# The sums of the down weights, made by GpSimd during the input projections instead of in prompt attention

## The reference, cut to what matters

```python
z = x @ w_in + b_in                       # GLU, q latent, kv latent, rope key, two gates
u, conv_state = causal_dwconv(conv_prev, a * sigmoid(g), conv_dw_w, conv_dw_b)   # width 31
y_conv = silu(layer_norm(u)) @ w_conv_out
...
mix = (g_conv * y_conv + g_mla * y_mla) @ w_mix_out   # y_mla: latent attention, prompt, then samples
x1 = layer_norm(ALPHA * x + mix)
h, ffn_state = causal_dwconv(ffn_prev, x1 @ w_up, ffn_dw_w, ffn_dw_b)            # width 3
f = (silu(hg) * hv) @ w_down              # w_down: 2816 x 1024
y = layer_norm(ALPHA * x1 + f)
```

## Time and profile before

| | |
|---|---|
| time, median of three runs | 2009.12 us (2006.18 to 2009.48) |
| the profiled execution's own time | 2004.44 us |
| its span, first to last instruction | 2002.6 us |
| mean granted clock of TensorE | 0.992 of full speed |
| busy in the span | PE 97%, PEld 89%, DVE 69%, ACT 42%, POOL 45% |
| moved by DMA | 264.08 MB, 132 GB/s on the mean |

### The profile page before, as it was taken

The page is one execution under the profiler, slowest core; times in us unless marked ns, Lnnn a source line. Parts: engine busy times, 40 slices in busy tenths (PEclk is TensorE's granted clock), DMA queues, the critical chain, the costliest instruction groups (busy, mean ns, idle before and its releaser), DMA issues.

```text
span 2002.6 us, 34425 instructions
## 1 busy us (share of the span) xinstructions
PE 1938.3 (97%) x13332; PEld 1782.6 (89%) x13332; DVE 1377.1 (69%) x1808; ACT 840.1 (42%) x1482; POOL 910.4 (45%) x562
## 2 busy tenths in 40 slices
PE   9999999999998999998999999989999999999998
PEld 8999999999997888886667999889999999977776
DVE  3999999956636647655445323798887777746778
ACT  4222222225335666674334121654544344554441
POOL 4812334421212343124330235678787878645542
PEclk9999999999999999999999999999999999999999
DMA  6422222323541333326573432242232222468655
GB/s 220 152 95 75 86 95 86 100 82 134 163 137 64 128 122 118 101 92 250 216 280 110 152 115 88 85 133 91 81 106 75 86 76 86 134 197 306 198 184 177
DMA packets 203535, 264.08 MB, mean 132 GB/s; under 512 B 22221, under 2 KB 142303, under 8 KB 199277
## 3 DMA queue, kind: packets, MB, share of 16 engines
q1 hardware_dynamic: 185600, 189.38, 29.6%
q0 software_dynamic: 8320, 46.27, 6.0%
q10 hardware_dynamic: 9469, 26.36, 3.5%
HBM read 200.25 MB, written 62.57 MB: 131 GB/s over the span
## 4 chain that ended last, share of the span: by engine, by line
PE 78%; DVE 10%; issue 3%; DMA 3%; ACT 3%; POOL 2%; SPq 1%; ACTq 0%; DVEq 0%; POOLq 0%
PE ps L2739 32%; PE ps L3394 14%; PE ps L3475 6%; PE ps L2932 5%; PE pst L3394 5%; PE pst L3475 2%; PE ps L3146 2%; PE ps L3199 1%; PE pst L3178 1%; DMA tw_d<-wraw 1%; PE pst L3011 1%; POOL tw_raw L1784 1%; DVE hv L2493 1%; PE pst L3181 1%; DVE tfr L2477 1%
## 5 line engine op out<-in xcount | busy, mean ns | idle before, releaser
L1710 POOL TENSOR_TENSOR wlo<-wraw,whi 128x1024 fp32r<-128x1024 f32 x66 | 160.4, 2435 | 388.2 <-ACT whi L981 293.3
L1986 DVE SCALAR_TENSOR_TENSOR pst<-g_ext,wtap,pst 128x512 f32<-128x512 f32 x464 | 306.9, 751 | 0.0
L2739 PE MATMUL ps<-xh,whi 128*128 128x352 f32 x864 | 187.1, 325 | 1.2 <-ACT stat L1075 1.2
L2739 PE MATMUL ps<-xh,wlo 128*128 128x352 f32 x864 | 186.2, 323 | 0.0
L2739 PE MATMUL ps<-xl,whi 128*128 128x352 f32 x864 | 186.0, 323 | 0.0
L2739 PEld LDWEIGHTS ps<-xh,whi 128*128 128x128 f32 x864 | 147.0, 189 | 1.9 <-issue 1.8
L2739 PEld LDWEIGHTS ps<-xh,wlo 128*128 128x128 f32 x864 | 148.3, 188 | 0.0
L2739 PEld LDWEIGHTS ps<-xl,whi 128*128 128x128 f32 x864 | 146.7, 188 | 0.0
L1880 POOL TENSOR_TENSOR wlo<-wraw,whi 128x512 fp32r<-128x512 f32 x60 | 90.8, 1520 | 33.1 <-ACT whi L1501 33.1
L1880 POOL TENSOR_TENSOR wlo<-x1f,whi 128x512 fp32r<-128x512 f32 x60 | 88.4, 1480 | 36.7 <-ACT whi L1501 36.7
L3394 PE MATMUL ps<-resr,whi 128*128 128x264 f32 x480 | 98.0, 286 | 0.0
(11 more groups left out here) (527 smaller groups left out, 5745.7 us busy)
## 6 DMA issues: line engine op xcount, KB each, us to landing
inr<-f_d SPq DMA_DIRECT2D x77, 256.0 KB, 4.1
wraw<-in_w_in SPq DMA_DIRECT2D x37, 512.0 KB, 3.8
f_d<-hv SPq DMA_DIRECT2D x22, 528.0 KB, 2.7
wraw<-in_w_up SPq DMA_DIRECT2D x40, 256.0 KB, 3.7
x1f<-in_w_up SPq DMA_DIRECT2D x40, 256.0 KB, 3.7
wraw<-in_w_down SPq DMA_DIRECT2D x27, 256.0 KB, 4.1
wraw<-tw_d SPq DMA_DIRECT2D x24, 256.0 KB, 3.8
tw_raw<-in_w_down SPq DMA_DIRECT2D x11, 512.0 KB, 3.5
```

The lines of the kernel that those rows point to most:

```text
L1710: nc.gpsimd.tensor_tensor(wlo[:, n % HL, :], wraw[:, n % RAW, :], whi[:, n % HL, :].bitcast(F32), ALU.subtract).then_inc(lo_done, 1)
L1986: half[x] = link(nc.vector.scalar_tensor_tensor(out=dst, in0=src, scalar=tap(k_), in1=pst[:, x, :], op0=ALU.mult, op1=ALU.add))
L2739: last = nc.tensor.matmul(out[:, c, 0:CH], w[:, k, :], x[:, k, c * CH:(c + 1) * CH], start=(k == 0 and x is hi_x and w is wh), stop=(k == ...
```

## The change

The sums move from prompt attention into the input projections. GpSimd makes those of two inner tiles in each tile m: k = 2m - 1 behind `lo(4m + 1)` and k = 2m behind `lo(4m + 3)`, from k = 0 at the end of tile 0 to k = 10 at the end of tile 5. The four subtractions are the same. The blocks lie in one buffer `tw` of four blocks, which covers the end of the place of `u`, the convolution's output (part of its tile 6 and its tile 7), so ScalarE now waits, in tile 6 before it writes the gate for VectorE, until all sums are stored. SyncE's loop over the tiles is written out, and in it loads (two transfers of 512 KB) and stores (one of 1 MB) stand between the loads of `w_in`. Semaphores that were shared with the old place are given back, and others are shared with the new one. In `tw_d` the four results have another order, which the loads of the down product follow.

```diff
-        tw_raw = at("tw_raw", [P, 2, NH], F32, X0 + 29568)
-        tw_low = wraw[:, (N2 + 1) % RAW, NH:2 * NH]
-        tw_high = at("tw_high", [P, NH], F32, R0 + 8192 + (N2 + 1) % HL * 4096 + 2048)
+        tw = at("tw", [P, 4, NH], F32, R1 + 2 * XB + 25600)
...
-            with sp.Fori(1, MT) as m:
+            w_dn = A["w_down"]
+
+            def w_down_blocks(k):
+                if k == 0:
+                    sp.wait_ge(tr_read, 1)
+                else:
+                    sp.wait_ge(ffn_out, 16 * k)
+                for j in range(2):
+                    r = (k + j * KH) * P
+                    sp.dma_start(tw[:, 2 * j:2 * j + 2, :], two(w_dn[0, r:r + P, :])).then_inc(gb2_in, 16)
+
+            def w_down_sums(k):
+                sp.wait_ge(xc_done, 4 * (k + 1))
+                sp.dma_start(tw_d[k].rearrange("j p n -> p j n"), tw[:, :, :]).then_inc(ffn_out, 16)
+
+            for m in range(1, MT):
                 for t in range(4):
-                    sp.wait_ge(lo_done, 4 * m + (t + 1))
-                    sp.dma_start(slot3(wraw, t % RAW), w_in_v[:, :, bass.ds(m * P + gate_cols[t], P)]
-                                 ).then_inc(raw_in[t % RAW], 16)
+                    load(4 * m + t, w_in_v[:, :, m * P + gate_cols[t]:(m + 1) * P + gate_cols[t]])
+                    k = 2 * (m - 1) + t // 2
+                    if k < KH:
+                        if t % 2:
+                            w_down_sums(k)
+                        else:
+                            w_down_blocks(k)
                 sp.wait_ge(wm_out, 16 * m)
-                sp.dma_start(wrow[:, :], A["w_mix_out"][0, bass.ds(m * P, P), :]).then_inc(wr_in, 16)
+                sp.dma_start(wrow[:, :], A["w_mix_out"][0, m * P:(m + 1) * P, :]).then_inc(wr_in, 16)
...
-                if h == 1:
-                    w_down_blocks(0)
-                if 1 <= h < 7:
-                    for k in range(2 * h - 2, min(2 * h, KH)):
-                        w_down_sums(k)
-                        if k + 1 < KH:
-                            w_down_blocks(k + 1)
-
-
-            sp.wait_ge(wm_out, TW_OUT)
...
-                    src = tw_d[k, {2: 0, 5: 1, 3: 2, 6: 3}[e]]
+                    src = tw_d[k, {2: 0, 5: 1, 6: 2, 3: 3}[e]]
...
                     elif t == 1:
+                        if m == MT - 2:
+                            act.wait_ge(ffn_out, TW_OUT)
                         nc.scalar.activation(split(sg[s][:, :]), acc(1), ACT.Sigmoid,
...
+            def w_down_sum(k, s, out, a, b):
+                if s < 2:
+                    pool.wait_ge(gb2_in, 32 * (k + 1))
+                else:
+                    pool.wait_ge(xc_done, 4 * k + s - (s == 2))
+                nc.gpsimd.tensor_tensor(out, a, b, ALU.subtract).then_inc(xc_done, 1)
+
+            def w_down_sums(k):
+                w11, w12, w21, w22 = (tw[:, j, :] for j in range(4))
+                w_down_sum(k, 0, w11, w12, w11)
+                w_down_sum(k, 1, w12, w22, w12)
+                w_down_sum(k, 2, w22, w22, w11)
+                w_down_sum(k, 3, w21, w21, w22)
+
             for m in range(MT):
                 for t in range(2):
                     lo(4 * m + t)
                     if m == 1:
                         x_tile(4 + t)
+                if 1 <= m < 6:
+                    w_down_sums(2 * m - 1)
...
                     if m == 1:
                         x_tile(6 + t)
+                if m < 6:
+                    w_down_sums(2 * m)
                 if m >= CSUM:
                     add_squares(max(1, m - 2))
...
-                if 1 <= h < 7:
-                    for k in range(2 * h - 2, min(2 * h, KH)):
-                        w_down_sums(k)
...
             pool.wait_ge(s_done, 8 * H)
-            pool.wait_ge(wm_out, TW_OUT)
```

More of the change, by code:

```diff
@@ L455, in program @@
         xb_in = sem("x_mean_in")
[L456 to L459, removed]
+        xc_done = sem("w_down_sum_steps_or_x_tile_centred")
+        wr_in = sem("w_mix_rows_in")
+        wm_c = sem("w_mix_centre_steps")
+        wm_out = sem("w_mix_rows_out")
         xr_out = sem("residual_stored")
@@ L471, in program @@
         f_in = x_in + ga_in + xt_in
-        gb2_in = sem("ln2_rows_in")
+        gb2_in = sem("w_down_blocks_or_ln2_rows_in")
         y_t = sem("down_product_tiles_done")
@@ L481, in program @@
         kf_r = sem("ffn_rows_read")
-        ffn_out = sem("ffn_state_out")
+        ffn_out = sem("w_down_sums_or_ffn_state_out")
         uses = [5, 4]
@@ L582, in program @@
         RS = {n: RS0 + j + 1 for j, n in enumerate(("11", "22", "samples", "12", "21"))}
-        TW_IN0, TW_C0, TW_OUT0 = 16 * MT, 3 * MT, 16 * MT
-        TW_OUT = TW_OUT0 + 48 * KH
+        TW_IN, TW_C, TW_OUT = 32 * KH, 4 * KH, 16 * KH
         UP_V0, UP_A0, F_HI0, F_LO0, SP_T0, SP_C0 = MT, MT, 2 * MT + 1, MT, 4, 6
@@ L710, in _ @@
             HQ = DN + DR
[L711 to L728, removed]
             for h in range(H):
@@ L969, in _ @@
             sp.wait_ge(orow_out[1], 32 * 4)
-            sp.wait_ge(ffn_out, 16 * (SG + 1))
+            sp.wait_ge(ffn_out, TW_OUT + 16 * (SG + 1))
             for j in range(4):
@@ L1777, in _ @@
                 lo(n)
-            def w_down_sum(k, s, out, a, b):
-                if s == 0:
-                    pool.wait_ge(wr_in, TW_IN0 + 48 * (k + 1))
-                elif s != 1:
-                    pool.wait_ge(wm_c, TW_C0 + 4 * k + (s - 1 if s == 2 else 3))
-                nc.gpsimd.tensor_tensor(out, a, b, ALU.subtract).then_inc(wm_c, 1)
-            def w_down_sums(k):
-                w_down_sum(k, 0, tw_raw[:, 0, :], tw_raw[:, 1, :], tw_raw[:, 0, :])
-                w_down_sum(k, 1, tw_raw[:, 1, :], tw_high[:, :], tw_raw[:, 1, :])
-                w_down_sum(k, 2, tw_high[:, :], tw_high[:, :], tw_raw[:, 0, :])
-                w_down_sum(k, 3, tw_low, tw_low, tw_high[:, :])
             for h in range(H):
@@ L2396, in _ @@
                 dve.wait_ge(w_used, N4 + m + HL + 1)
-                dve.wait_ge(xc_done, m + 1)
+                dve.wait_ge(xc_done, TW_C + m + 1)
                 residual(m, None, None).then_inc(free[q], 1)
@@ L2673, in normalise @@
                 if t == Y_TURN[0]:
-                    dve.wait_ge(gb2_in, 32)
+                    dve.wait_ge(gb2_in, TW_IN + 32)
                 if t == 8:
```

## The result

The changed kernel takes 1986.76 us (median of 4 runs, 1984.52 to 1989.37) against 2007.65 (2005.18 to 2009.48) for the kernel before, run beside it: a ratio of 0.9901, 95% interval [0.9888, 0.9914]. Two more sets of runs gave 0.9900 and 0.9906. So it is faster, as forecast, but by 20.9 us where 12.3 was forecast, and 1986.76 lies under the range of 1992 to 2004. In the changed kernel the lines of TensorE and VectorE are 10 lower, those of ScalarE and GpSimd 6 to 13.

What follows compares the result with a forecast made beforehand. TensorE, busy 97% of the span, was taken as the bound. Stalls of 7.87 us plus slower stretches of 4.39 us, nothing added, came off the 2009.12 us median: 1996.8 us, with 1992 to 2004 for 8 in 10.

Steps and rivals of the forecast that it cites:

- the change, part by part: Whole kernel: costs what leaves attention (44 subtractions, 33 loads, 33 stores) and what joins the input projections; 12.26 us saved, nothing added.
- The two terms: Prompt attention: TensorE's three `pbuf` stalls return, 7.87 us, and the longer stretches after the first two return, 4.39 us.
- the prediction's list of four waits: Prompt attention: TensorE waited four times for ScalarE's `pbuf`, 8.3 us in all and 2.9 us at most.
- The first rival: Prompt attention: TensorE's clock falls and VectorE's rope steps are late as before; 7.87 us saved, 2001.2 us; chance 0.13.
- VectorE falls behind: Input tiles: GpSimd's sums hold VectorE through the shared port, 45 us at worst, 2028.5 us; chance 0.05 of being slower.
- A weight tile late: Input projections: first sums held, `lo(4)` and `lo(6)` past their margins, products wait say 5 us, 2002 us; chance 0.04.
- the margin's prediction: Input projections: after one sum `lo(4)` ends at 64.7, 2.9 us before product 4; each further microsecond would lengthen the end.
- Another wait takes the place: Prompt attention: ScalarE's own work around the stalls is the limit, so nothing is gained, 2009 us; chance 0.06.
- 5 to 8 us late at no cost: Input stage: VectorE expected 5 to 8 us late, covered by 13.4 us of room before TensorE needs it.
- its signs of being wrong: TensorE waits for `wlo` between 60 and 120 us or for VectorE near 434, or the three stalls remain behind another releaser.
- the bound of 5.2: Input tile 1: one run of sums can hold VectorE by at most GpSimd's own four instructions, 5.2 us.
- the 5.8 us of room at the gate: Input tiles: VectorE waited 1.45 us for the gate in tile 4 and the three after, 5.8 us able to absorb lateness.

Runs made afterwards that it cites:

- E1: Kernel before, with SyncE issuing the first 1 MB of down-weight blocks only after five of six kr rows are stored: 2000.48 us against 2005.42, ratio 0.9973.
- E2: Kernel before, sums still in attention, with SyncE issuing each next head's loads ahead of the stores of the sums: 1994.32 us, ratio 0.9939.
- E3: Kernel before, with first blocks after the small stores and each head's loads ahead of the sums, all sums still in attention: 1988.89 us, ratio 0.9915.
- E9: Kernel before, first blocks later, head loads ahead, and in heads 2 and 4 the second sum held until VectorE's `qsr` copies: 1984.31 us, ratio 0.9896.
- E4: Changed kernel, with the 1 MB load of the first blocks put back at its old place, into buffers nobody reads: 1992.15 us, 0.9933 of the kernel before.
- E5: Changed kernel, with four GpSimd subtractions without transfers put back into attention in heads 2, 4 and 6: 1989.88 us against 1986.06 for the changed kernel.
- E6: Changed kernel, with each sum's four subtractions made twice in the input stage: 1998.0 us, 0.996 of the kernel before.
- E7: Changed kernel without the 44 GpSimd subtractions in the input stage, blocks still loaded and stored as they are: 1985.56 us, 0.9896 of the kernel before.

## Why the prediction came short

The lengths of the pairs, each from its first `whi` x `ckvh` to that of the next, side by side; the first column is from TensorE's first product `ckvh` x `whi` (at 603.88 before) to the first of these (us):

```
                              to pair 1   pair 1   pair 2   pair 3
before                             4.48    80.81    77.17    74.57
E1 first blocks later              2.85    81.06    76.98    76.03
E2 loads ahead of the sums         4.40    77.56    73.10    71.31
E3 both                            2.84    77.60    73.12    71.32
E9 both, clear of the rope         2.86    75.25    71.53    71.47
changed                            2.88    75.27    71.47    71.46
E4 changed + first load            4.44    75.08    71.47    71.47
E5 changed + 4 subtractions        2.84    76.75    72.87    72.85
```

**The step that failed** is the first of "the change, part by part": of what is removed from attention, 33 loads and 33 stores were costed by SyncE's waits and the three stalls in the pairs alone. The first load, which is issued before any pair, was never looked up, nor the wait of 3.73 us at 603.88. It was TensorE's longest in attention. Its price is 3.73 − 0.51 = 3.22 us of wait and 4.48 − 2.88 = 1.60 us at the lower clock, 4.8 us; E1 measured 4.9, E4 5.4.

The other 0.7 of the 5.54 lies ahead of attention, and the change didn't earn it. With VectorE late, TensorE's first product for the sums over the channels starts 0.97 us later (435.46, before 434.49); yet VectorE's `qrf` starts 0.71 us earlier (595.19, before 595.90). The 1.7 us between came from TensorE's clock, which in the profiled execution of the kernel before was at the lower level for longer; first before, then changed:

```profile
435.00:445.00 10.00, 10.00 (x66) 10.00 (x66) 0.89 (x5) 2.32 (x3) 0.00 (x0) 0.66 0.13 54
```

```profile
435.00:445.00 10.00, 9.54 (x74) 9.54 (x75) 1.30 (x6) 2.54 (x4) 2.52 (x1) 0.83 0.34 108
```

E1, E2, E3 and E9 have the input stage of the kernel before, and in this window E1 and E2 have 0.66, E3 and E9 0.83: it is luck of the execution.

So the rows give the change 14.35 + 4.8 − 1.0 = 18.2 us (three pairs, first load, VectorE's lateness), and the medians of the first runs are 20.9 apart. The rest isn't shown, as one execution of the kernel before was profiled. One candidate: in E1 the third stall, of 2.78 us, did cost clock, and its pair lasted 76.03 us, 1.5 more than in that execution. And the forecast was set against 2009.12 us, where the kernel before took 2007.65 beside the changed one; 1.5 us of the miss are this mark.

**The two terms** were right in kind and 2.1 us small: 4.88, 4.91 and 2.47 us were forecast for the pairs, and 5.54, 5.70 and 3.11 came. The yardstick was at fault: the third pair of before, taken as free of losses but for its stall of 2.47 us, lost 0.64 us more. It had lost all of it by the second wait for `pbuf` behind that stall, which the prediction's list of four waits had and its sum of three left out; first before, then changed:

```profile
817.00 0.77 PE L3011 MATMUL pst<-ident,pbuf 128*128 128x128 f32 x5 [0.40 <-ACT pbuf L1277]
```

```profile
797.10 0.77 PE L3001 MATMUL pst<-ident,pbuf 128*128 128x128 f32 x5 [0.26 <-ACT pbuf L1266]
```

The two kernels are 766.34 − 749.56 = 16.78 us apart where this pair begins, 817.00 − 797.10 = 19.90 here, and 19.89 where it ends. So a stall without loss of clock cost 3.1 us and not the 2.47 of its idle time, and with the loads ahead of the sums the pair lasts 71.31 us (E2). The same 0.6 to 0.8 is missing in each pair. By the experiments the order of the queue gave 10.6 us (E2), stalls and clock together, and the sums beside the rope 2.29 and 1.63 us; these two are of E2, where TensorE waits longer for `ptl` than the 1.17 and 1.16 us of the kernel before, so they don't divide the losses of that kernel.

**The first rival**, that only the stalls return, fell: clock and rope copies came back, as E2 and E5 show one by one. The second, *VectorE falls behind*, asked for 25.7 us of lateness to be slower at all; 8.4 came. *Another wait takes the place* fell too: the pairs ran without the stalls, so ScalarE had the room. *A weight tile late* didn't come, and E6 shows how near it was: with 5.17 us more for each inner tile TensorE waited 2.46 us for `lo(4)`, where 5.17 − 2.9 = 2.3 was the margin's prediction.

**VectorE** was to be 5 to 8 us late at no cost. It was 8.4 late at its last step (434.16 against 425.75), and TensorE waited 0.69 us for it, which the prediction had among its signs of being wrong. The last add of x and sum 2 held it 5.3 us, near the bound of 5.2; what was missed is that `lo(8)` and `lo(9)`, pushed back by the sums, now run beside VectorE's next steps (`prod` 3.28 us, 2.1 more), and that the 5.8 us of room at the gate would be used up by another step: from tile 3 on the bias step, late, ran beside GpSimd's squares, at 1.34 and 0.76 us in tiles 3 and 4 and 1.77 in tiles 5 to 7, in place of 0.23. E7 shows VectorE on time without the subtractions. The taps from PSUM stayed at 737 to 751 ns, as the earlier trace rows had it.

## What to carry to other kernels

When a step is moved away, list every transfer that it issued at its old place, the first one too, and look in the trace for what else was in flight there: the longest wait of the stage may be a small store beside it, charged to another engine. A yardstick interval has losses of its own; check its waits before taking a difference to it. And when a move pays, try the cheap cause at the old place: one wait and a changed order of issue gave 16.5 of some 20 us (E3), one wait more the rest (E9).

## What the runs showed of the hardware

- An 8 KB store took 5.3 us from issue to landing beside 1 MB of loads on another queue (the kernel before, E4), and 2.0 to 2.6 us without them (E1, the changed kernel).
- The clock doesn't follow a stall's length: in the kernel before, stalls of 2.88 and 2.52 us were followed by 0.83 over the window and one of 2.47 by 1.00; in E1 those of 2.59 and 2.78 were followed by 0.83 and that of 3.12 by 1.00. The levels behind such a mean are 1.2 and 2.4 GHz.
- A VectorE copy of 31 columns that began beside GpSimd was held 6.02 us, past the ends of three GpSimd instructions, and 4.00 us when GpSimd paused earlier. The Trainium skill, "SBUF — State Buffer", section "Who interferes with whom", says that where GpSimd and a VectorE instruction in a two-port mode meet, whoever issues first has the shared port pair for the whole instruction while the other blocks fully. E5's rows agree, copies ending with single subtractions. The 6.02 us do not follow from it: by that rule the copy would have begun when the add ended, at 100.15, and been over some 2.4 us after its start, an estimate from the 0.18 us that it takes in the later tiles.
